# Second feed-forward: the down phase's second pass over 512 tokens becomes two passes over 256 tokens, and two more output tiles are finished under the last

## The chip, the cores and the metric

The kernel runs on one core of one Trainium2 chip. The metric is device time in microseconds (us): 3741.64 us median of 3 runs, 3740.01 to 3745.3. Engines are named as in the profile: PE (matrix multiplies), PEld (its weight loads), DVE (vector), ACT (scalar), POOL, and SP, the queue that issues the DMAs.

## The reference, cut to what matters

The program is a stack of two attention layers and a conditioned block of four stages. Only the last stage is touched: the second conv feed-forward, with its normalised, gated residual.

```python
D_MODEL, SEQ, D_FF = 1024, 1024, 2816
def conv_ffn(h, w_up, conv_w, conv_b, w_down):
    u = h @ w_up
    gate, val = u[..., :D_FF], u[..., D_FF:]
    gp = jnp.pad(gate, ((0, 0), (1, 1), (0, 0)))
    gate = gp[:, :-2] * conv_w[0] + gp[:, 1:-1] * conv_w[1] + gp[:, 2:] * conv_w[2] + conv_b
    return (jax.nn.silu(gate) * val) @ w_down
# end of the second block, per token:
x = x + gate_f * rmsnorm_2(conv_ffn(h, w_up[i], conv_w[i], conv_b[i], w_down[i]), g_post_ffn[i])
```

All of it is float32. The down product is hidden (1024 tokens by 2816) times w_down (2816 by 1024).

## The kernel before, in words

2816 is 22 chunks of 128 (`FT` = 22). The up phase computes each chunk of hidden, 128 channels by 1024 tokens, and stores it to memory outside the core (`hidden_dram`). The down phase reads it back and multiplies. A float32 operand is split into a high and a low part that the matrix unit takes, and a product is three matmuls: high by high, high by low, low by high.

**The down phase before** is two passes (h = 0, 1) over all 22 chunks. Pass h covers 512 tokens, that is 4 token tiles of 128, and both 512-column halves of the output; its 8 accumulators fill the 8 banks of `core.ps`. One step (h, f) is:
- SP loads chunk f of w_down (`down_raw`, 128 x 1024, 512 KB, L1793) and 512 tokens of hidden chunk f (`h_raw`, called hidden_columns in the trace, 256 KB, L1794). There are two slots for everything; s = f % 2.
- ACT copies both into high parts (`down_hi` L1888, `h_hi` L1889).
- DVE subtracts to get the low parts (`down_lo` L1972, `h_lo` L1974).
- PE runs 8 banks x 3 = 24 matmuls of 128x512 (L2070 to L2072).

**What sets the order.** The load for step n waits until DVE has finished the low parts of step n-2 (`down_lo` in `sync`), since these still read the raw slot. ACT's split of step n waits for both transfers of step n, and for PE to have finished step n-2 (`up_used`, or `acc` where n-2 ends a pass). PE's step n waits for DVE's low parts of step n. Every engine runs its instructions in program order. At a pass's end ACT evicts the even banks and DVE the odd ones into `y` (called x in the trace, L1941 and L2029); the next pass's first step waits for the eviction of each bank that it writes.

**The tail, class `Final`.** Each of 8 token tiles needs: ACT's sum of squares and mean (L2347, L2349), POOL's power -1/2 (L2363), DVE's scale (L2381) and addition of the old rows (L2383), and SP's store (L2331). Tiles 0 to 3 (`EARLY` = 4), complete after pass 0, are done in pass 1: ACT and POOL at steps 8 to 11, DVE at 10 to 13, the stores at 18 to 21. SP also loads the factor row at step 0 and one tile of old rows (512 KB each, L2324) at each of steps 0 to 7. Tiles 4 to 7 come after the last matmul.

Of the kernel before, what the change touches and what calls it, by code (L numbers as in the profile page):

```python
# [19 lines left out]
P = 128  # L20
# [1698 lines left out]
class FeedForward:  # L1719
# [12 lines left out]

    def __init__(self, core, combined, base, x_at, y, w_up, w_down, conv, hidden_dram, tail):
        self.core, self.combined, self.y, self.w_up, self.w_down = core, combined, y, w_up, w_down
# [43 lines left out]
    def sync(self, sp):  # L1778
        core, combined, cv, stored, final = self.core, self.combined, self.cv, self.stored, self.final

        def step(sp, f, s):
            if not final(f):
                sp.wait_ge(core.up_lo.sem, core.up_lo.at(3 * f + 3))
                combined.load(sp, self.w_up, f + 1)
            if not isinstance(f, int) or f > 0:
                sp.wait_ge(core.hidden.sem, core.hidden.at(f))
                sp.dma_start(self.hidden_dram[f - 1], cv[:, 1 - s]).then_inc(stored[1 - s].sem, 16)
        self.walk(sp, step)
        sp.wait_ge(core.up_lo.sem, core.up_lo.at(3 * FT))
# [12 lines left out]
        def down(h, f, s):  # L1802
            if h == 0 and isinstance(f, int) and f == FT - 2:
                sp.wait_ge(core.stored0.sem, core.stored0.at(8 * FT))
            if h == 0 and final(f):
                sp.wait_ge(core.stored1.sem, core.stored1.at(8 * FT))
            if h == 1 or not isinstance(f, int) or f > 1:
                sp.wait_ge(core.down_lo.sem, core.down_lo.at(2 * (h * FT + f) - 2))
                load(h, f, s)
        self.walk(sp, lambda sp, f, s: down(0, f, s))  # L1810
        for f in range(FT):
            down(1, f, f % 2)
            core.enter(self.tail.mark)
            self.tail.sync_early(sp, f)
            core.enter(self.mark)

# [25 lines left out]
    def gpsimd(self, pool):  # L1842
# [7 lines left out]
        self.walk(pool, step)  # L1850
        for f in range(FT):
            core.enter(self.tail.mark)
            self.tail.gpsimd_early(pool, f)
            core.enter(self.mark)
# [22 lines left out]
    def scalar(self, act):  # L1877
# [3 lines left out]
        def split(h, f, s):  # L1881
            n = h * FT + f
            act.wait_ge(downs[s].sem, downs[s].at(16 * (n - s) + 32))
            if h == 1 and isinstance(f, int) and f == 1:
                act.wait_ge(core.acc.sem, core.acc.at(8))
            else:
                need(act, core.up_used, FT - 1 if isinstance(f, int) and n == FT else n - 1 - h)
# [37 lines left out]
        def down(h, f, s):  # L1925
            if not final(f):
                split(h, f + 1, 1 - s)
            elif h == 0:
                split(1, 0, 0)
        for h in range(2):  # L1930
            if h == 0:
                self.walk(act, lambda act, f, s: down(0, f, s))
            else:
                for f in range(FT):
                    down(1, f, f % 2)
                    core.enter(self.tail.mark)
                    self.tail.scalar_early(act, f)
                    core.enter(self.mark)
            for b in range(0, 8, 2):
                act.wait_ge(core.acc.sem, core.acc.at(8 * h + b + 1))  # L1940
                act.activation(self.y[:, 4 * h + b // 2, 0:512], core.ps[:, b, :], ACT.Copy).then_inc(core.acc_used_act.sem, 1)  # L1941

# [21 lines left out]
    def vector(self, dve):  # L1964
# [4 lines left out]
        def split(h, f, s):  # L1969
# [3 lines left out]
            dve.wait_ge(core.down_hi.sem, core.down_hi.at(2 * n + 2))  # L1973
            dve.tensor_tensor(self.h_lo[:, s], self.h_raw[:, s], self.h_hi[:, s].bitcast(F32), ALU.subtract).then_inc(core.down_lo.sem, 1)  # L1974

# [37 lines left out]
        def down(h, f, s):  # L2013
            if not final(f):
                split(h, f + 1, 1 - s)
            elif h == 0:
                split(1, 0, 0)
        for h in range(2):
            if h == 0:
                self.walk(dve, lambda dve, f, s: down(0, f, s))  # L2020
            else:
                for f in range(FT):
                    down(1, f, f % 2)
                    core.enter(self.tail.mark)
                    self.tail.vector_early(dve, f)
                    core.enter(self.mark)
            for b in range(1, 8, 2):
                dve.wait_ge(core.acc.sem, core.acc.at(8 * h + b + 1))
                dve.tensor_copy(self.y[:, 4 * h + b // 2, 512:D], core.ps[:, b, :]).then_inc(core.acc_used_dve.sem, 1)  # L2029

    def tensor(self, pe):
# [25 lines left out]
        self.walk(pe, step)  # L2057
        for h in range(2):
            def down(pe, f, s):
                pe.wait_ge(core.down_lo.sem, core.down_lo.at(2 * (h * FT + f) + 2))  # L2060
                begin, end = isinstance(f, int) and f == 0, final(f)
                for b in range(8):
                    if begin and h == 0 and b % 4 == 0:
                        pe.wait_ge(core.parts_act.sem, core.parts_act.at(3 * (FT - 1 + b // 4)))
                        pe.wait_ge(core.parts_dve.sem, core.parts_dve.at(5 * (FT - 1 + b // 4)))
                    if begin and h == 1:
# [12 lines left out]
    def passed(self):  # L2079
        core = self.core  # L2080
        for c, n in ((core.raw0, 16 * FT), (core.up_hi, 3 * FT), (core.up_lo, 3 * FT), (core.weight_sums, 4 * FT), (core.products, 7 * FT),
                     (core.parts_act, 3 * FT), (core.parts_dve, 5 * FT), (core.gate_mid, FT), (core.gate_used, 2 * FT), (core.expo, FT),
                     (core.hidden, FT), (core.stored0, 8 * FT), (core.stored1, 8 * FT), (core.raw2, 32 * FT), (core.raw3, 32 * FT),
                     (core.down_hi, 4 * FT), (core.down_lo, 4 * FT), (core.up_used, 2 * (FT - 1)), (core.acc, 16),
                     (core.acc_used_act, 8), (core.acc_used_dve, 8)):
# [220 lines left out]
class Final:  # L2306

    def __init__(self, core, base, X, kept, factor_row, out):  # L2310
        self.core, self.X, self.kept, self.factor_row, self.out = core, X, kept, factor_row, out
# [6 lines left out]
    def sync_early(self, sp, f):  # L2318
# [14 lines left out]
    def sync(self, sp):  # L2333
        core = self.core
        for m in range(EARLY, TILES):
            self.store(sp, m)
# [14 lines left out]
    def scalar_early(self, act, f):  # L2351
        if 8 <= f < 8 + EARLY:
            self.scalar_tile(act, f - 8)

    def scalar(self, act):
        for m in range(EARLY, TILES):
            self.scalar_tile(act, m)
# [7 lines left out]
    def gpsimd_early(self, pool, f):  # L2365
        if 8 <= f < 8 + EARLY:
            self.gpsimd_tile(pool, f - 8)

    def gpsimd(self, pool):
        for m in range(EARLY, TILES):  # L2370
            self.gpsimd_tile(pool, m)
# [13 lines left out]
    def vector_early(self, dve, f):  # L2385
        if 10 <= f < 10 + EARLY:
            self.vector_tile(dve, f - 10)

    def vector(self, dve):
        for m in range(EARLY, TILES):  # L2390
            self.vector_tile(dve, m)
# [1004 lines left out]
def build(nc, I, out, stop=None):  # L3396

    with ExitStack() as ctx:
# [131 lines left out]

        def feed_forward(i, tail):
            conv = vec[:, VECTORS[f"conv{i}"]:VECTORS[f"conv{i}"] + 4 * FT].rearrange("p (a f) -> p a f", a=4)
            return FeedForward(core, combined[i], base, x_at, X, I["w_up"][i], I["w_down"][i], conv, hidden_dram, tail)
# [136 lines left out]
```

## Time and profile before

| | |
|---|---|
| median of 3 runs | 3741.64 us |
| profiled execution's own time | 3741.64 us |
| its span, first to last instruction | 3741.6 us |
| PE busy | 3430.4 us, 92% of the span |
| DVE, ACT, POOL busy | 2225.6, 1742.0, 1372.9 us |
| moved from and to memory | 269.76 MB read, 61.10 MB written |

The span and the profiled execution's own time agree, so a microsecond in the trace is one in the metric. Only the last 240 us are touched: the down phase of the second feed-forward runs from about 3484 to 3726 us, and the tail from there to the end. Matmuls are pipelined: one of 128x512 lasts 0.39 us in the trace, but the next starts 0.23 us after it, and that distance is what counts for a stream.

### The profile page before, as it was taken

Reading aid. Unit: us, or ns where it says so; the run is one execution under the profiler, and the core shown is the slowest. Engines: PE = TensorE matmul, PEld = TensorE weight load, DVE = VectorE, ACT = ScalarE, POOL = GpSimd, SP = SyncE. Lnnn points to the kernel's source line nnn. Section 1 sums busy time; section 2 is a strip of 40 time slices with the busy share of each in tenths; the row PEclk is TensorE's granted clock in tenths of the full one; section 3 lists DMA queues with packets and bytes.
Section 4 is the critical chain, followed back from the end, with each engine's and each line's share of the span. In section 5 each row is a group of like instructions: output and inputs, shape, how many; then the busy total and the mean of one; then the engine's idle time right before and its main releaser. Section 6 shows DMA issues by size and latency. Waiting matters only on the chain. (4 is left out here: it accounts for less than half of the span.)

```text
span 3741.6 us, 59020 instructions
## 1 busy us (share of the span) xinstructions
PE 3430.4 (92%) x18578; PEld 3015.6 (81%) x18578; DVE 2225.6 (59%) x4539; ACT 1742.0 (47%) x4132; POOL 1372.9 (37%) x1819
## 2 busy tenths in 40 slices
PE   5899989899999999797999939999998969999998
PEld 4799867899999997686998728888787758888786
DVE  5466777455677776435887186666435566666334
ACT  1277511767877772323665153333333463333333
POOL 2365433455566773313332224444001214444000
PEclk8999989999999998898999959999999779999999
DMA  3311255211212214300000022222364012222454
GB/s 137 140 39 41 97 230 225 88 43 42 60 60 64 64 61 169 131 1 29 1 0 0 34 107 85 84 80 83 126 205 140 34 57 80 80 82 84 138 194 146
DMA packets 97326, 332.99 MB, mean 89 GB/s; under 512 B 10705, under 2 KB 37633, under 8 KB 85122
## 3 DMA queue, kind: packets, MB, share of 16 engines
q1 hardware_dynamic: 97154, 330.90, 25.0%
q8 instruction: 83, 1.36, 0.2%
q14 instruction: 89, 0.73, 0.1%
HBM read 269.76 MB, written 61.10 MB: 88 GB/s over the span
## 5 line engine op out<-in xcount | busy, mean ns | idle before, releaser
L2070 PE MATMUL ps<-down_high,hidden_high 128*128 128x512 f32 x704 | 276.8, 393 | 15.0 <-DVE hidden_low L1974 14.6
L2071 PE MATMUL ps<-down_low,hidden_high 128*128 128x512 f32 x704 | 275.6, 391 | 0.0
L2072 PE MATMUL ps<-down_high,hidden_low 128*128 128x512 f32 x704 | 275.5, 391 | 0.0
L376 PE MATMUL ps<-w_hi,hT_hi 128*128 128x512 f32 x640 | 254.6, 398 | 22.0 <-DVE hT_lo L401 11.7
L1972 DVE TENSOR_TENSOR down_low<-down_raw,down_high 128x1024 fp32r<-128x1024 f32 x88 | 107.8, 1225 | 272.4 <-ACT down_high L1888 272.4
L2053 PE MATMUL ps<-columns_combined,up_high_even 128*128 128x512 f32 x616 | 242.6, 394 | 22.2 <-DVE columns_combined L2259 8.0
L377 PE MATMUL ps<-w_lo,hT_hi 128*128 128x512 f32 x640 | 253.4, 396 | 0.0
L378 PE MATMUL ps<-w_hi,hT_lo 128*128 128x512 f32 x640 | 253.0, 395 | 0.0
L2054 PE MATMUL ps<-columns_combined,up_high_even 128*128 128x512 f32 x616 | 241.8, 393 | 0.0
L2055 PE MATMUL ps<-columns_combined,up_low_even 128*128 128x512 f32 x616 | 241.6, 392 | 0.0
L2053 PE MATMUL ps<-columns_combined,up_high_odd 128*128 128x512 f32 x616 | 239.6, 389 | 0.0
L2054 PE MATMUL ps<-columns_combined,up_high_odd 128*128 128x512 f32 x616 | 239.6, 389 | 0.0
L2055 PE MATMUL ps<-columns_combined,up_low_odd 128*128 128x512 f32 x616 | 239.6, 389 | 0.0
L1092 ACT ACTIVATE masked_then_probs<-masked_then_probs,unit_rows 128x256 f32<-128x256 f32 (+1 forms) x512 | 229.1, 451 | 3.2 <-DVE sink_term L1179 1.8
L1888 ACT ACTIVATE down_high<-down_raw 128x1024 fp32r<-128x1024 f32 x88 | 93.1, 1058 | 269.3 <-PE ps L2072 256.4
L974 PE MATMUL ps<-w_units,hT_hi 128*128 128x384 f32 (+1 forms) x512 | 184.6, 361 | 22.3 <-DVE w_units L1138 16.6
L1029 PEld LDWEIGHTS ps<-v_tiles,probsT 128*128 128x128 f32 x1600 | 200.1, 195 | 1.4 <-issue 1.4
L976 PE MATMUL ps<-w_units,hT_lo 128*128 128x384 f32 (+1 forms) x576 | 198.9, 345 | 0.0
L1029 PE MATMUL ps<-v_tiles,probsT 128*128 128x64 f32 x1600 | 196.6, 274 | 0.8 <-DVE unit_rows L1252 0.8
L1170 DVE CUSTOM_DVE_ANT_0 masked_then_probs<-ps,mask 128x256 f32<-128x256 f32 (+1 forms) x512 | 156.1, 359 | 58.9 <-PE ps L991 58.6
L2491 DVE SCALAR_TENSOR_TENSOR mod_sums<-mod_weights,silu_c,mod_sums 128x512 f32 x196 | 182.4, 942 | 6.0
L974 PE MATMUL ps<-w_units,hT_hi_by_fours 128*128 128x384 f32 (+1 forms) x512 | 183.6, 359 | 0.0
(367 smaller groups left out, 9941.9 us busy)
## 6 DMA issues: line engine op xcount, KB each, us to landing
mod_weights<-in_w_mod SPq DMA_DIRECT2D x24, 2048.0 KB, 9.0
up_raw<-in_w_up SPq DMA_DIRECT2D x44, 1024.0 KB, 4.8
down_raw<-in_w_down SPq DMA_DIRECT2D x88, 512.0 KB, 3.6
hidden_columns<-hidden SPq DMA_DIRECT2D x44, 512.0 KB, 2.6
hidden_columns<-hidden_columns SPq DMA_DIRECT2D x88, 256.0 KB, 3.9
w_raw<-in_w_in_b SPq DMA_DIRECT2D x24, 768.0 KB, 4.5
group_rows<-unit_rows SPq DMA_DIRECT2D x64, 132.0 KB, 1.8
unit_rows<-group_rows SPq DMA_DIRECT2D x64, 132.0 KB, 2.1
```

Source lines behind the costliest of these rows:

```text
L376: nc.tensor.matmul(out, a, w_hi[:, s], start=(k == 0), stop=False)
L377: nc.tensor.matmul(out, a, w_lo[:, s], start=False, stop=False)
L378: last = nc.tensor.matmul(out, b, w_hi[:, s], start=False, stop=(k == KT - 1))
L974: nc.tensor.matmul(zbank, hi, weights(w_hi, a.unit, k), start=(k == 0), stop=False)
L1029: last = nc.tensor.matmul(o_bank[:, h * HD:(h + 1) * HD], pT[:, a.par, h, c], vs[:, tile], start=(c == a.slots[0]), stop=(c == a.slots[-1]))
L1092: act.activation(x, x, ACT.Exp, bias=own, scale=-1.0, accum_out=total).then_inc(core.probs.sem, 1)
L2053: nc.tensor.matmul(out, a_hi, combined.moving(0, z, k), start=(start and k == 0), stop=False, **again)
L2054: nc.tensor.matmul(out, a_hi, combined.moving(1, z, k), start=False, stop=False, **again)
L2055: last = nc.tensor.matmul(out, a_lo, combined.moving(0, z, k), start=False, stop=(k == 3), **again)
L2070: nc.tensor.matmul(out, h_hi[:, s, t], down_hi[:, s, cols], start=begin, stop=False)
L2071: nc.tensor.matmul(out, h_hi[:, s, t], down_lo[:, s, cols], start=False, stop=False)
L2072: last = nc.tensor.matmul(out, h_lo[:, s, t], down_hi[:, s, cols], start=False, stop=end)
```

## The change

The second feed-forward gets three passes instead of two. Pass 0 is as it was. Pass 1 covers tokens 512 to 767 in banks 0 to 3, pass 2 covers tokens 768 to 1023 in banks 4 to 7. Each of them walks all 22 chunks again: it loads the whole of chunk f of w_down and 256 tokens of hidden, splits them, and runs 12 matmuls a step. The steps of both are numbered through for the tail, 0 to 43. Tiles 4 and 5, complete after pass 1, are finished in pass 2: ACT and POOL at its steps 5 and 6, DVE at 7 and 8, the stores at 13 and 14. Tiles 6 and 7 remain for the end (`LATE` = 6). The first feed-forward keeps its two passes. Accumulators are counted so that pass 2 finds banks 4 to 7 evicted since pass 0.

```diff
+    HALVES = ((0, 512, 0, 8), (512, 512, 0, 8))
+    LAST_QUARTERS = ((0, 512, 0, 8), (512, 256, 0, 4), (768, 256, 4, 8))
...
             sp.dma_start(self.down_raw[:, s], self.w_down[f]).then_inc(self.downs[s].sem, 16)
-            sp.dma_start(self.h_raw[:, s], self.hidden_dram[f][:, 512 * h:512 * h + 512]).then_inc(self.downs[s].sem, 16)
+            first, n = self.passes[h][:2]
+            sp.dma_start(self.h_raw[:, s, 0:n], self.hidden_dram[f][:, first:first + n]).then_inc(self.downs[s].sem, 16)
...
-            if h == 1 or not isinstance(f, int) or f > 1:
+            if h >= 1 or not isinstance(f, int) or f > 1:
                 sp.wait_ge(core.down_lo.sem, core.down_lo.at(2 * (h * FT + f) - 2))
                 load(h, f, s)
         self.walk(sp, lambda sp, f, s: down(0, f, s))
-        for f in range(FT):
-            down(1, f, f % 2)
-            core.enter(self.tail.mark)
-            self.tail.sync_early(sp, f)
-            core.enter(self.mark)
+        for h in range(1, len(self.passes)):
+            for f in range(FT):
+                down(h, f, f % 2)
+                core.enter(self.tail.mark)
+                self.tail.sync_early(sp, (h - 1) * FT + f)
+                core.enter(self.mark)
...
-            if h == 1 and isinstance(f, int) and f == 1:
-                act.wait_ge(core.acc.sem, core.acc.at(8))
+            if h >= 1 and isinstance(f, int) and f == 1:
+                act.wait_ge(core.acc.sem, core.acc.at((8, 12)[h - 1]))
...
-            act.activation(self.h_hi[:, s], self.h_raw[:, s], ACT.Copy).then_inc(core.down_hi.sem, 1)
+            tokens = slice(0, self.passes[h][1])
+            act.activation(self.h_hi[:, s, tokens], self.h_raw[:, s, tokens], ACT.Copy).then_inc(core.down_hi.sem, 1)
...
-                for b in range(8):
+                for b in range(low, high):
...
-                    out, t, cols = core.ps[:, b, :], slice((b // 2) * P, (b // 2) * P + P), slice((b % 2) * 512, (b % 2) * 512 + 512)
+                    m = (b - low) // 2
+                    out, t, cols = core.ps[:, b, :], slice(m * P, m * P + P), slice((b % 2) * 512, (b % 2) * 512 + 512)
...
+    LATE = 6
...
-        if f >= FT - EARLY:
+        if FT - EARLY <= f < FT:
             self.store(sp, f - (FT - EARLY))
+        if f - FT in (13, 14):
+            self.store(sp, f - FT - 13 + EARLY)
...
+        if f - FT in (5, 6):
+            self.scalar_tile(act, f - FT - 5 + EARLY)
...
+        if f - FT in (7, 8):
+            self.vector_tile(dve, f - FT - 7 + EARLY)
...
-        second = feed_forward(1, final)
+        second = feed_forward(1, final, FeedForward.LAST_QUARTERS)
```

DVE's low parts and the evictions are cut to the pass's tokens and banks in the same way, and POOL's tiles 4 and 5 are placed as ACT's are.

**SP's queue** around the last steps of pass 1 (down_raw and hidden_columns are a step's two loads, out_x is the store of a finished tile). Before:

```order
L2331 DMA out_x<-x 128x1024 [waits x_new]
L1793 DMA down_raw_21217<-in_w_down 128x1024 [waits down_lo]
L1794 DMA hidden_columns_21220<-hidden_columns 128x512
L2331 DMA out_x<-x 128x1024 [waits x_new] x5
L3352 UNCONDITIONAL_BRANCH [waits loads]
```

The same place now, and the first steps of pass 2 behind it:

```order
L2345 DMA out_x<-x 128x1024 [waits x_new]
L1797 DMA down_raw_21217<-in_w_down 128x1024 [waits down_lo]
L1799 DMA hidden_columns_21220<-hidden_columns 128x256
L1797 DMA down_raw_21217<-in_w_down 128x1024 [waits down_lo]
L1799 DMA hidden_columns_21220<-hidden_columns 128x256
```

Before, five stores and the end followed the last load; now 22 more pairs of loads follow the fourth store, and each pair waits for DVE's low parts of two steps earlier. The weight load kept its width, the token load has half.

**DVE's queue** at the end of the program (COPY is an eviction, the two rows behind it are the scale and the addition of one tile). Before:

```order
L1972 TENSOR_TENSOR down_low_21219<-down_raw_21217,down_high_21218 128x1024 [waits down_hi]
L1974 TENSOR_TENSOR hidden_low_21222<-hidden_columns_21220,hidden_high_21221 128x512 [waits down_hi]
L2029 COPY x<-ps 128x512 [waits acc] x4
L2381 SCALAR_TENSOR_TENSOR x<-x,statistics,final_factor 128x1024 [waits y_rstd,ready1]
L2383 TENSOR_TENSOR x<-x,final_old_rows 128x1024 [waits y_scaled]
```

And the end of the first of the two short passes, where DVE has two evictions, with the next pass behind it:

```order
L1979 TENSOR_TENSOR down_low_21219<-down_raw_21217,down_high_21218 128x1024 [waits down_hi]
L1982 TENSOR_TENSOR hidden_low_21222<-hidden_columns_21220,hidden_high_21221 128x256 [waits down_hi]
L2037 COPY x<-ps 128x512 [waits acc] x2
L1979 TENSOR_TENSOR down_low_21219<-down_raw_21217,down_high_21218 128x1024 [waits down_hi]
L1982 TENSOR_TENSOR hidden_low_21222<-hidden_columns_21220,hidden_high_21221 128x256 [waits down_hi]
```

Before, the four evictions were followed by four tiles of two instructions each (the fence shows the first); now two evictions stand in the middle and two at the end, two tiles have moved up into pass 2, and two are left behind the last eviction.

## Rows read from the trace of the kernel before

**Rows 1.** Table by stretches: PE busy (instructions), granted clock, DMA share, GB/s
```profile
core 0: us, PE busy (x), PEclk, DMA share, GB/s
3500.00:3594.00 94.00, 94.00 (x416) 1.00 0.44 148
3600.00:3632.00 32.00, 32.00 (x143) 1.00 0.73 250
...
3607.00:3726.00 119.00, 119.00 (x527) 1.00 0.52 174
```

**Rows 2.** The chain that ended last: start, length, what
```profile
3725.94 0.04 ACT x L1941
3725.99 0.45 issue
3726.44 1.15 ACT final_squares L2347 x2
...
3728.70 1.29 DVE x L2381
...
3737.38 1.22 DVE x L2383
```

**Rows 3.** Timeline of SP, two issues of the loads
```profile
3642.59 0.33 SPq L1793 DMA_DIRECT2D down_raw<-in_w_down  x1
3642.96 0.43 SPq L1794 DMA_DIRECT2D hidden_columns<-hidden_columns  x1
```

**Rows 4.** Timeline of ACT, same step
```profile
3639.64 1.06 ACT L1888 ACTIVATE down_high<-down_raw 128x1024 fp32r<-128x1024 f32 x1 [3.86 <-PE ps L2072]
3640.61 0.61 ACT L1889 ACTIVATE hidden_high<-hidden_columns 128x512 fp32r<-128x512 f32 x1
3645.08 1.06 ACT L1888 ACTIVATE down_high<-down_raw 128x1024 fp32r<-128x1024 f32 x1 [3.86 <-PE ps L2072]
```

**Rows 5.** Timeline of DVE, the same step, and one with a tile
```profile
3640.73 1.23 DVE L1972 TENSOR_TENSOR down_low<-down_raw,down_high 128x1024 fp32r<-128x1024 f32 x1 [3.61 <-ACT down_high L1888]
3641.88 0.68 DVE L1974 TENSOR_TENSOR hidden_low<-hidden_columns,hidden_high 128x512 fp32r<-128x512 f32 x1
...
3664.24 1.28 DVE L2381 SCALAR_TENSOR_TENSOR x<-x,statistics,final_factor 128x1024 f32<-128x1024 f32 x1
3665.55 1.22 DVE L2383 TENSOR_TENSOR x<-x,final_old_rows 128x1024 f32<-128x1024 f32 x1
```

**Rows 6.** Landing of the 39 weight loads L1793, from 3500 us on
```profile
L1793 SPq DMA_DIRECT2D down_raw<-in_w_down x39: 327/328/339, 3500.1 to 3707.9; - x39
...
DMA to landing us min/median/max: 3.2/3.6/4.1
```

**Rows 7.** Landing of the 39 token loads L1794, from 3500 us on
```profile
L1794 SPq DMA_DIRECT2D hidden_columns<-hidden_columns x39: 332/433/598, 3500.6 to 3708.2; - x39
...
DMA to landing us min/median/max: 3.5/3.9/4.9
```

**Rows 8.** The chain of waits where pass 0 starts
```profile
3490.34 4.43 DMA hidden_columns<-hidden_columns
3494.77 0.02 issue
3494.79 1.07 ACT down_high L1888
3495.86 0.02 issue
3495.89 0.57 DVE down_low L1972
...
3497.03 0.69 DVE hidden_low L1974
3497.72 0.04 issue
3497.77 0.50 PE ps L2070
```

**Rows 9.** Table by stretches, a crowded queue, and PE with gaps at either clock
```profile
412.00:429.00 17.00, 13.60 (x113) 1.00 0.08 25
1842.00:1853.00 11.00, 9.47 (x68) 1.00 0.00 0
3059.40:3064.30 4.90, 4.90 (x12) 0.50 0.00 0
3489.80:3496.40 6.60, 6.12 (x27) 1.00 0.92 318
```

More of the change, by code:

```diff
@@ L1731, with __init__ @@
              (6, 2, 2, False, 2), (3, 4, 3, True, 3))
-    def __init__(self, core, combined, base, x_at, y, w_up, w_down, conv, hidden_dram, tail):
+    HALVES = ((0, 512, 0, 8), (512, 512, 0, 8))
+    LAST_QUARTERS = ((0, 512, 0, 8), (512, 256, 0, 4), (768, 256, 4, 8))
+    def __init__(self, core, combined, base, x_at, y, w_up, w_down, conv, hidden_dram, tail, passes=HALVES):
+        self.passes = passes
         self.core, self.combined, self.y, self.w_up, self.w_down = core, combined, y, w_up, w_down
@@ L1850, in gpsimd @@
         self.walk(pool, step)
-        for f in range(FT):
+        for f in range((len(self.passes) - 1) * FT):
             core.enter(self.tail.mark)
@@ L1927, in down @@
                 split(h, f + 1, 1 - s)
-            elif h == 0:
-                split(1, 0, 0)
-        for h in range(2):
+            elif h < len(self.passes) - 1:
+                split(h + 1, 0, 0)
+        for h, (first, n, low, high) in enumerate(self.passes):
             if h == 0:
@@ L1934, in scalar @@
                 for f in range(FT):
-                    down(1, f, f % 2)
+                    down(h, f, f % 2)
                     core.enter(self.tail.mark)
-                    self.tail.scalar_early(act, f)
+                    self.tail.scalar_early(act, (h - 1) * FT + f)
                     core.enter(self.mark)
-            for b in range(0, 8, 2):
-                act.wait_ge(core.acc.sem, core.acc.at(8 * h + b + 1))
-                act.activation(self.y[:, 4 * h + b // 2, 0:512], core.ps[:, b, :], ACT.Copy).then_inc(core.acc_used_act.sem, 1)
+            for b in range(low, high, 2):
+                act.wait_ge(core.acc.sem, core.acc.at((8 if h else 0) + b + 1))
+                act.activation(self.y[:, first // P + (b - low) // 2, 0:512], core.ps[:, b, :], ACT.Copy).then_inc(core.acc_used_act.sem, 1)
     def first_sums(self, dve, early=False):
@@ L1973, in split @@
             dve.wait_ge(core.down_hi.sem, core.down_hi.at(2 * n + 2))
-            dve.tensor_tensor(self.h_lo[:, s], self.h_raw[:, s], self.h_hi[:, s].bitcast(F32), ALU.subtract).then_inc(core.down_lo.sem, 1)
+            tokens = slice(0, self.passes[h][1])
+            dve.tensor_tensor(self.h_lo[:, s, tokens], self.h_raw[:, s, tokens], self.h_hi[:, s, tokens].bitcast(F32), ALU.subtract).then_inc(core.down_lo.sem, 1)
         def step(dve, f, s):
@@ L2015, in down @@
                 split(h, f + 1, 1 - s)
-            elif h == 0:
-                split(1, 0, 0)
-        for h in range(2):
+            elif h < len(self.passes) - 1:
+                split(h + 1, 0, 0)
+        for h, (first, n, low, high) in enumerate(self.passes):
             if h == 0:
@@ L2022, in vector @@
                 for f in range(FT):
-                    down(1, f, f % 2)
+                    down(h, f, f % 2)
                     core.enter(self.tail.mark)
-                    self.tail.vector_early(dve, f)
+                    self.tail.vector_early(dve, (h - 1) * FT + f)
                     core.enter(self.mark)
-            for b in range(1, 8, 2):
-                dve.wait_ge(core.acc.sem, core.acc.at(8 * h + b + 1))
-                dve.tensor_copy(self.y[:, 4 * h + b // 2, 512:D], core.ps[:, b, :]).then_inc(core.acc_used_dve.sem, 1)
+            for b in range(low + 1, high, 2):
+                dve.wait_ge(core.acc.sem, core.acc.at((8 if h else 0) + b + 1))
+                dve.tensor_copy(self.y[:, first // P + (b - low) // 2, 512:D], core.ps[:, b, :]).then_inc(core.acc_used_dve.sem, 1)
     def tensor(self, pe):
@@ L2057, in tensor @@
         self.walk(pe, step)
-        for h in range(2):
+        for h, (first, n, low, high) in enumerate(self.passes):
             def down(pe, f, s):
@@ L2334, in sync @@
         core = self.core
-        for m in range(EARLY, TILES):
+        for m in range(self.LATE, TILES):
             self.store(sp, m)
@@ L2353, in scalar_early @@
             self.scalar_tile(act, f - 8)
+        if f - FT in (5, 6):
+            self.scalar_tile(act, f - FT - 5 + EARLY)
     def scalar(self, act):
-        for m in range(EARLY, TILES):
+        for m in range(self.LATE, TILES):
             self.scalar_tile(act, m)
@@ L2367, in gpsimd_early @@
             self.gpsimd_tile(pool, f - 8)
+        if f - FT in (5, 6):
+            self.gpsimd_tile(pool, f - FT - 5 + EARLY)
     def gpsimd(self, pool):
-        for m in range(EARLY, TILES):
+        for m in range(self.LATE, TILES):
             self.gpsimd_tile(pool, m)
@@ L2387, in vector_early @@
             self.vector_tile(dve, f - 10)
+        if f - FT in (7, 8):
+            self.vector_tile(dve, f - FT - 7 + EARLY)
     def vector(self, dve):
-        for m in range(EARLY, TILES):
+        for m in range(self.LATE, TILES):
             self.vector_tile(dve, m)
@@ L3529, in build, with feed_forward @@
         combined = [Combined(core, base) for _ in range(2)]
-        def feed_forward(i, tail):
+        def feed_forward(i, tail, passes=FeedForward.HALVES):
             conv = vec[:, VECTORS[f"conv{i}"]:VECTORS[f"conv{i}"] + 4 * FT].rearrange("p (a f) -> p a f", a=4)
-            return FeedForward(core, combined[i], base, x_at, X, I["w_up"][i], I["w_down"][i], conv, hidden_dram, tail)
+            return FeedForward(core, combined[i], base, x_at, X, I["w_up"][i], I["w_down"][i], conv, hidden_dram, tail, passes)
         final = Final(core, base, X, x_dram, rows_dram[4], out)
-        second = feed_forward(1, final)
+        second = feed_forward(1, final, FeedForward.LAST_QUARTERS)
         pool = PoolMix(core, base, x_at, X, x_dram, rows_dram, I, pre_ffn[1][:], mod[1][:, 24:32], second)
```

9 lines of the change are left out of this document (5 added, 4 removed).

## Prediction

> **What bounds the kernel now.** I read first the table by stretches, since the change touches only the last 240 us. In it the reader is to see that PE is busy for the whole of each stretch, 94.00 of 94.00 and 119.00 of 119.00 us, at clock 1.00 [rows 1]. So the down phase is bound by PE alone: 527 matmuls in 119 us are 0.226 us each, a step of 24 is 5.44 us, and pass 1 is 22 x 5.44 = 119.7 us. Then the chain that ended last: after the last evictions it holds only the tail, ACT's squares from 3726.44, DVE's first scale at 3728.70, then eight DVE instructions back to back until 3738.6 [rows 2], and the last store, with the span's end at 3741.6. One tile costs DVE 3664.24 to 3665.55 and some 1.15 more, 2.45 us [rows 5]; in the tail the last addition starts at 3737.38 and the first scale at 3728.70, which gives (3737.38 + 1.22 - 3728.70)/4 = 2.475 a tile [rows 2]. Last, what feeds PE: the timelines of SP, ACT and DVE for one step and the landings of its two transfers [rows 3 to 7]. There ACT and DVE wait 3.86 and 3.61 us per step, ACT for PE: everything that prepares a step has slack today, because PE takes 5.44 us for it. That slack is what the change spends.
>
> **The tail: a gain of 4.9 us.** Four tiles behind the last eviction become two. ACT's last eviction, its squares, POOL and DVE's first scale follow each other as now, so the start of DVE's run keeps its distance from the last matmul, and its run is two tiles shorter: 2 x 2.475 = 4.9 us. The last store lands 3.0 us after DVE as now (3741.6 - 3738.6).
>
> **PE's own work: zero.** 44 steps of 12 matmuls are the 528 of 22 steps of 24. Pass 2 writes banks 4 to 7, evicted since pass 0, so it waits for no eviction. If PE were still the bound, these passes would again take 119.7 us.
>
> **Feeding PE: the large term.** A step now lasts PE 12 x 0.227 = 2.72 us, but it still needs the whole 512 KB of w_down, ACT's 128x1024 copy and DVE's 128x1024 subtraction. Only the token part is halved. With two slots the load of step n+2 is issued when DVE has finished the low parts of step n, so one turn of a slot is a closed loop in which PE has no part:
> - DVE's end to SP's issue: 3641.88 + 0.68 = 3642.56 to 3642.59, 0.03 us [rows 5, 3].
> - Issue to both landed: the weights land 3.6 us after their issue [rows 6]. The tokens are issued 0.37 later [rows 3] and land 3.9 after that [rows 7], at 4.27. So the 256 KB add 0.67, and I take half of it for 128 KB: 3.6 + 0.33 = 3.93.
> - Landing to ACT's copy 0.02 [rows 8]; ACT's start to DVE's start 3640.73 - 3639.64 = 1.09 [rows 4, 5]; DVE's first subtraction to its second 1.15 [rows 5].
> - The second subtraction has 256 columns. From 1.23 us for 1024 columns and 0.68 for 512 [rows 5] the slope is 0.55 per 512, so 0.68 - 0.27 = 0.41.
>
> The turn is 0.03 + 3.93 + 0.02 + 1.09 + 1.15 + 0.41 = 6.63 us for two steps, 3.3 a step where PE needs 2.72. The loop was there before, with 6.63 + 0.34 + 0.27 = 7.24 us for two steps, under PE's 10.88. That it can be last is seen where pass 0 starts: the chain runs through the transfer (4.43 us), ACT, DVE, PE [rows 8].
>
> Bounds of the landing: the least token landing is 3.5 and the greatest 4.9 [rows 7], so both have landed after 3.5 + 0.37 - 0.33 = 3.54 or 4.94, which is 6.24 or 7.64 a turn, 3.12 or 3.82 a step. If halving the tokens saves nothing, 4.27 gives 3.5. I take the median, 3.3.
>
> **The sum of the two passes.** Steps 0 to 2 were fed during pass 0 and run at PE's pace, 8.2 us; the load of step 3 needs the low parts of step 1, which need the last matmul of pass 0: 2.7 (ACT and DVE) + 3.95 (landing) + 2.7 = 9.4 us until PE starts step 3. The 40 intervals to the start of step 43 at 3.31 are 132.6, the last step 2.7: together 144.7. On top:
> - DVE in the six steps with a tile: 1.15 + 0.33 (0.41 less the 0.08 by which DVE's instructions overlap, 1.23 against 1.15) + 2.45 = 3.93, longer than 3.31, with the next subtraction queued behind the tile and SP's next load waiting for it: 6 x 0.62 = 3.7 us.
> - The transfers of old rows at pass 1's steps 0 to 7: a step moves 512 + 128 + 512 KB, 1.18 MB. In the crowded stretch the queue moved 318 GB/s [rows 9], so 3.7 us a step, 0.4 above 3.31. Before, the same extras were hidden: PE 32.00 of 32.00 us at 250 GB/s [rows 1]. Six intervals lie behind step 3: 2.4 us. The six stores are as large; I take half of their 2.4, since a transfer to memory delays only the weights behind it: 1.2.
>
> That is 144.7 + 3.7 + 2.4 + 1.2 = 152.0 us against 119.7: a loss of 32.3. With the tail: 32.3 - 4.9 = +27.4. The profiled execution took 3741.6 us, the same as the median, so 3741.6 + 27.4 = 3769; the queue's extras may partly coincide with DVE's, so I forecast 3768 us.
>
> A page bears on the landing. "DMA: Bandwidth & Descriptors", section "Anatomy of one DMA", of the Trainium skill gives some 2.0 us fixed plus bytes over 436 GB/s; for this pair of 655,360 bytes an estimate by it is 3.5 us in place of 3.93, 6.2 us a turn, and about 3760 us. It was fitted on another engine's path, and by it the pair of today, 786,432 bytes, would land after 3.8 where the rows show 4.27; the rows decide.
>
> **Rivals.**
> 1. **The loads stay hidden, PE stays the bound.** The two passes take 119.7 us and the tail's 4.9 come off whole: 3736.7, and with one start-up gap of 1.2 (9.4 - 8.2) about 3738, faster. For it: PE never waits in either pass today [rows 1], and the queue's share is 0.44 to 0.52. It needs a turn below 5.44 us. Against it: without any transfer the turn is 2.7 us, so the pair would have to land within 2.74 us of its issue, and the fastest of 39 weight loads alone took 3.2 [rows 6]. Chance 4%.
> 2. **Crowded queue.** If every transfer lands as late as the latest today, 3.82 a step: 9.4 + 152.8 + 2.7 + 3 = 167.9, that is +43.3, 3785. For it: twice the weight bytes per us, some 640 KB in 3.3 us, 200 GB/s against 148 in quiet steps [rows 1]. Against it: at 250 GB/s PE did not wait at all, and 318 were reached. Chance 12%.
> 3. **PE's clock falls.** With gaps of 0.6 us in every 3.3, PE is busy for 82%. At the lower level 12 matmuls filled 4.9 us at a granted 0.50 [rows 9], so the half level of 1.2 GHz makes PE the bound again: 44 x 4.9 = 216, and 3741.6 + 216 - 119.7 - 4.9 = 3833. Against it: with 13.60 of 17.00 us busy, 80%, and 9.47 of 11.00, the clock stayed at 1.00 [rows 9]. Chance 4%. "TensorE: Matmul & The Clock Gate", section "HAM oscillation", of the Trainium skill speaks for this rival: matmul bursts with waits for transfers between them can each start at the half clock. The waits here are shorter than in its example, and the rows above show none of it.
> 4. **The loop at its best.** 3.12 a step and no extra but DVE's: 9.4 + 124.8 + 2.7 + 3.7 = 140.6, +16, 3757.6. Chance 15%.
>
> **How the numbers follow.** The forecast, the loop of load, ACT, DVE and load at about 3.3 us a step, has 65%, with 3761 to 3776 as its own range; the rivals above have 35%. The range is 3755 to 3782: it takes in the best loop and most of the way to the crowded queue, and leaves out rival 1, rival 3 and the worst of rival 2. A measurement of this kernel tells about 0.2%, 7.5 us. Only rival 1 ends below or near the old time: 2% for faster by more than that, 2% for within it (rival 1's 3738 lies inside 0.2%, but without the start-up gap and with a little more from the tail it may reach beyond), 96% for slower.
>
> **What would show it.** In the changed profile: PE waits at the first matmul of nearly every step of passes 1 and 2 for DVE's hidden_low; ACT's down_high waits for the transfer and no longer for PE; steps are 3.1 to 3.5 us apart, 3.7 to 3.9 where a tile or old rows are; PE's clock stays at 1.00; first DVE scale of the last tiles some 2.3 us behind the last matmul as now, and two tiles, not four, behind it. I am wrong if ACT still waits for PE in these passes, if the weights land under 2.7 us, or if the granted clock falls.

## The result and the profile after

| | before | changed |
|---|---|---|
| median | 3741.34 us (4 runs, 3740.01 to 3745.3) | 3771.23 us (4 runs, 3767.9 to 3773.41) |
| profiled span | 3741.6 us | 3766.1 us |
| PE busy | 3430.4 us | 3436.6 us |
| read from memory | 269.76 MB | 281.29 MB |

The ratio is 1.0078, 95% interval 1.0064 to 1.0093: 30 us slower, where the forecast was 3768 us in 3755 to 3782. A second set of five runs beside other runs of the kernel before gave 3771.36 us and 1.0081 (1.0068 to 1.0095). One of the ten executions of a variant below (e6) took 12320.87 us at a mean granted clock of 0.267; it is left out, and e6's median is that of the other nine.

One correction to the table before: in every later profiled execution the time is about 1.8 us above the span (3767.9 and 3766.1), so equal numbers for the kernel before are doubtful by as much. Stretches of the trace are safer than spans here. Nothing ahead of pass 1 was changed, yet in the profiles below that leave pass 0 alone its last eviction starts anywhere between 3598.9 and 3609.2 us. I therefore measure passes 1 and 2 from the start of DVE's last eviction of pass 0 to the start of its last of all. In the timeline of DVE (start, length, what, and in brackets the wait before it and what ended it) the kernel before has

```profile
3606.94 0.69 DVE L2029 COPY x<-ps 128x512 f32<-128x512 f32 x1 [0.38 <-PE ps L2072]
...
3726.62 0.69 DVE L2029 COPY x<-ps 128x512 f32<-128x512 f32 x1 [0.67 <-PE ps L2072]
```

and the changed kernel

```profile
3604.40 0.69 DVE L2037 COPY x<-ps 128x512 f32<-128x512 f32 x1 [0.65 <-PE ps L2081]
...
3756.06 0.69 DVE L2037 COPY x<-ps 128x512 f32<-128x512 f32 x1 [0.69 <-PE ps L2081]
```

That is 119.68 us against 151.66, a loss of 31.98. Below, "the passes" is always this stretch. The tail from there, in the chain that ended last:

```profile
3755.87 1.15 ACT final_squares L2361 x2
...
3758.06 1.29 DVE x L2399
3759.38 1.23 DVE x L2401
3760.61 1.21 DVE x L2399
3761.84 1.23 DVE x L2401
```

Four DVE instructions in the chain where there were eight [rows 2]. From that last eviction to the span's end it is 3766.1 - 3756.06 = 10.0 us, before it was 3741.6 - 3726.62 = 15.0. Read to the end of DVE's last addition, in hundredths, it is 7.01 us against 11.98 [rows 2], which is 4.97 less. The two stretches together give 31.98 - 4.97 = +27.0 us.

Where the 32 us went is shown by the table of waits inside the passes (who waited for whom: total us, times, longest):

```profile
ACT down_high L1894 <- DMA hidden_columns<-hidden_columns: 78.0, 40, 3.0
PE ps L2079 <- DVE hidden_low L1982: 20.5, 29, 1.3
ACT down_high L1894 <- PE ps L2081: 1.4, 1, 1.4
```

ACT waits 40 times for the transfer and once for PE; before it waited for PE, 3.86 us a step [rows 4]. And the chain that ended last, which held only PE in this stretch before, is now the slot's loop (start, length, what):

```profile
3733.35 0.33 SPq L1797
...
3733.72 3.40 DMA hidden_columns<-hidden_columns
...
3737.14 1.07 ACT down_high L1894
...
3738.23 1.23 DVE down_low L1979
3739.46 0.35 DVE hidden_low L1982
3739.82 0.33 SPq L1797
...
3746.45 0.33 SPq L1797
```

The same slot's load is issued at 3733.35, 3739.82 and 3746.45: 6.47 and 6.63 us for two steps, with PE nowhere in them. I call this distance, from the issue of the weights of step n to that of step n+2, the turn of step n (steps 0 to 43 of passes 1 and 2). Some turns hold extra work, and I group them by it: 3 to 9 lie beside the loads of old rows, 12 to 15 and 31, 32 behind a tile on DVE, 19 to 23 and 36 to 38 beside a store. The 18 others from 3 to 41 I call plain. The two slots turn independently, so the steps are not evenly spaced: behind step 3 the issues follow each other after 2.4 to 4.4 us. The table by stretches answers to [rows 1]:

```profile
core 0: us, PE busy (x) PEld busy (x) DVE busy (x) ACT busy (x) POOL busy (x), PEclk, DMA share, GB/s
3606.00:3757.00 151.00, 129.30 (x521) 94.36 (x519) 83.23 (x102) 68.44 (x108) 4.15 (x6) 1.00 0.68 218
```

PE is busy 129.30 of 151 us, at the full clock of 2.4 GHz (granted 1.00) throughout.

### The profile page after: what moved, and what is told of

Same layout as the page of the kernel before. It is cut to its first block and busy times, and to the rows that moved or that the text cites. A ratio compares the mean times of both kernels' runs of the same rounds, so it can differ in the third digit from the quotient of the medians.

```text
span 3766.1 us, 59212 instructions
## 1 busy us (share of the span) xinstructions
PE 3436.6 (91%) x18578; PEld 3009.3 (80%) x18578; DVE 2255.8 (60%) x4583; ACT 1766.6 (47%) x4176; POOL 1368.9 (36%) x1819
## 3 DMA queue, kind: packets, MB, share of 16 engines
HBM read 281.29 MB, written 61.10 MB: 91 GB/s over the span
## 5 line engine op out<-in xcount | busy, mean ns | idle before, releaser
L1979 DVE TENSOR_TENSOR down_low<-down_raw,down_high 128x1024 fp32r<-128x1024 f32 x110 | 134.7, 1225 | 274.9 <-ACT down_high L1894 274.9
L1894 ACT ACTIVATE down_high<-down_raw 128x1024 fp32r<-128x1024 f32 x110 | 116.4, 1059 | 277.0 <-PE ps L2081 184.6
L2079 PEld LDWEIGHTS ps<-down_high,hidden_high 128*128 128x128 f32 x704 | 133.2, 189 | 83.0 <-DVE hidden_low L1982 55.4
```

## The experiments

All start from the changed kernel. Passes are in us from one profile each. Two variants do not compute the product any more: e2 multiplies whatever weights the slots still hold, and e9 multiplies tokens 512 to 767 again in pass 2.

| run | edit | passes | median, ratio to before (interval) |
|---|---|---|---|
| changed, a2 | none | 151.66 and 152.80 | 3771.23, 1.0078 (1.0064 to 1.0093); 3771.36, 1.0081 (1.0068 to 1.0095) |
| e1 | tiles 4, 5 at the end | 151.57 | 3772.31, 1.0079 (1.0064 to 1.0094) |
| e2 | no weights loaded | 134.04 | 3751.12, 1.0022 (1.0012 to 1.0032) |
| e3 | three raw slots | 134.13 | 3752.12, 1.0027 (1.0017 to 1.0038) |
| e4 | old rows in pass 0 | 151.87 | 3770.69, 1.0075 (1.0059 to 1.009) |
| e5 | half tiles | 152.97 | 3771.21, 1.0076 (1.0061 to 1.0091) |
| e8 | e4 and e5 | 146.77 | 3765.18, 1.0061 (1.0046 to 1.0077) |
| e9 | 512 tokens loaded | 161.20 | 3780.65, 1.0101 (1.0086 to 1.0117) |
| e10 | tokens counted apart | 147.72 | 3764.55, 1.006 (1.0044 to 1.0075) |
| e6 | three slots for loads and parts | 122.80 | 3740.42, 0.9996 (0.9986 to 1.0006) |
| e7 | e6, e4, e5 | 120.12 and 121.70 | 3738.47, 0.9989 (0.998 to 0.9998); 3737.75, 0.9984 (0.9975 to 0.9993) |

### a2: the changed kernel again

No edit; it gives the spread of one profile.

> The changed kernel once more, on the same chip as the next three, to have its passes and its time beside theirs. Passes 1 and 2, from the last eviction of pass 0 to the last eviction of the end, took 151.7 us in its first profile: between 150 and 153 again, tail 10.5 us, about 27 us slower than the kernel before.

The passes took 3756.18 - 3603.38 = 152.80 us, 1.1 more than in the first profile, and 3766.2 - 3756.18 = 10.0 us lie behind them. Below, differences under 2 us between single profiles say nothing.

### e1: the tail alone

```diff
-    LATE = 6
+    LATE = 4
...
-        if f - FT in (7, 8):
-            self.vector_tile(dve, f - FT - 7 + EARLY)
```

with the tiles' ACT, POOL and store calls taken out in the same way.

> The changed kernel with tiles 4 and 5 finished at the end again, behind the last matmul. Theory (slot loop plus a shorter tail): the tail is 4.9 us longer, two of the six steps that DVE stretches to 3.93 us are back at 3.3 (-1.2), so 3.7 us slower than the changed kernel, about 3775 us; between DVE's first scale of the end and its last addition 9.8 us instead of 4.9. Rival (the work moved under the pass costs there as much as it saves at the end): no difference, 3771.

In the chain of waits of this run the tail is

```profile
3757.88 1.29 DVE x L2393
...
3766.55 1.22 DVE x L2395
```

eight instructions, 3766.55 + 1.22 - 3757.88 = 9.89 us against 5.01 in the changed kernel (3758.06 to 3763.07). So the move is worth 4.9 us at the end. The rival was that the two tiles cost as much under pass 2. Then e1's passes would be 4.9 us shorter than the changed kernel's; they took 151.57 us against 151.66 and, in a2, 152.80. The 1.2 us that they were to lose did not show in the sum either. It shows in the turns: those of steps 31 and 32, behind the two tiles, took 7.59 and 7.85 us and now 6.59 and 6.60, which is 1.1 us over both, since a turn covers two steps. In this one profile the turns beside old rows and stores were slower by more than that (7.37 and 7.23 us on the mean against 7.06 and 7.05 in the first profile). The time was expected at 3775 us; the medians (3772.3 and 3771.2, from different chips) do not resolve 5 us between them, and the trace does.

### e2: without the weights' transfer

```diff
-            sp.dma_start(self.down_raw[:, s], self.w_down[f]).then_inc(self.downs[s].sem, 16)
+            if not short:
+                sp.dma_start(self.down_raw[:, s], self.w_down[f]).then_inc(self.downs[s].sem, 16)
```

> The changed kernel, but passes 1 and 2 load only the 256 tokens of a step (128 KB) and no weights: the 512 KB of w_down are left out, everything else runs on what the slots hold. Theory (the weights' transfer is the long part of the slot's turn): a landing of about 2.2 us instead of 3.93 makes the turn 4.9 us, under PE's 5.44, so steps of 2.8 us, 3.9 where DVE has a tile: the two passes take about 128 us instead of 149, time about 3750. Rival A (ACT's and DVE's preparation of a step is the bound, whatever the transfer): no change, 3771. Rival B (PE itself is slowed by waiting and restarting at each step): no change either, steps stay at 3.3.

The 40 token loads landed in

```profile
DMA to landing us min/median/max: 2.2/2.3/2.5
```

and the passes fell from 152 to 134.04 us. The median fell to 3751, as expected, but the passes were expected at 128; the plain turns are 5.83 us here as in e3, where the reason shows. In the waits ACT waited for PE again, 36 times between 3608 and 3726 us. So ACT's and DVE's preparation is not the bound at 3.3 us a step, and PE's restarts are not either: the transfer is the long part of the loop.

### e3: the same bytes, a third raw slot

```diff
+            self.down_raw_third = place("down_raw_third", [P, D], F32, base + 11 * RKB)
+            self.h_raw_third = place("hidden_columns_third", [P, 512], F32, base + 12 * RKB)
...
-                sp.wait_ge(core.down_lo.sem, core.down_lo.at(2 * (h * FT + f) - 2))
+                sp.wait_ge(core.down_lo.sem, core.down_lo.at(2 * (h * FT + f) - (4 if h and len(self.passes) == 3 else 2)))
```

> The changed kernel with a third slot for the loaded data of passes 1 and 2 (weights and tokens); high and low parts keep two slots. The same bytes are moved. Theory (a closed loop of load, ACT, DVE with two slots, bound by latency): the turn of 6.6 us now covers three steps, 2.2 a step, so the next bound shows: ACT may write the high parts of step n+2 only when PE is done with step n, 2.85 + 2.72 us for two steps, 2.8 a step; with 3.7 where old rows are loaded (8 steps) and 3.9 at DVE's tiles (6 steps) the passes take about 137 us instead of 149: time about 3759. Rival (the queue is bound by bytes, 640 KB in 3.3 us): the same bytes in the same time, no change, 3771.

The passes took 134.13 us, the same as without the weights. Over the passes the queue moved 240 GB/s where it had 221, so bytes did not bind in the changed kernel. What bound was the length of the loop, divided by only two slots. In the timeline of ACT the next bound shows:

```profile
3607.50 1.06 ACT L1913 ACTIVATE down_high<-down_raw 128x1024 fp32r<-128x1024 f32 x1 [1.35 <-PE ps L2101]
...
3610.61 1.06 ACT L1913 ACTIVATE down_high<-down_raw 128x1024 fp32r<-128x1024 f32 x1 [1.74 <-PE ps L2101]
...
3613.33 1.06 ACT L1913 ACTIVATE down_high<-down_raw_third 128x1024 fp32r<-128x1024 f32 x1 [1.35 <-PE ps L2101]
```

Steps are 3.11 and 2.72 us apart in turn, and ACT waits for PE each time: 5.83 us for two steps, where I had reckoned 5.57. This next loop is ACT, DVE, then PE's step, then ACT again. The chain that ended last shows which part I had too short:

```profile
3712.80 1.07 ACT down_high L1913
...
3715.51 0.50 PE ps L2099
...
3718.67 1.07 ACT down_high L1913
```

From ACT's start to PE's first matmul it is 2.71 us (reckoned 2.85), but from there to ACT's next start 3.16, where I had put PE's 2.72. In PE's timeline the first two matmuls after the wait are 0.34 us apart and the twelfth starts 2.67 us after the first, in place of 11 x 0.227 = 2.50; it then lasts its full 0.40 us before ACT may start. The steps with old rows, which I had put at 3.7 us, run at this same pace, so that the passes came out at 134 us and not at the 137 expected.

### e4, e5 and e8: the two extras

e4 calls `old_rows(sp, f - 4)` after each step of pass 0 instead of in pass 1. e5 splits a tile:

```diff
-        if 10 <= f < 10 + EARLY:
-            self.vector_tile(dve, f - 10)
...
+        if 10 <= f < 10 + 2 * EARLY:
+            self.vector_tile(dve, (f - 10) // 2, f % 2)
...
```

The last argument chooses the half: the scale in one step, the addition in the next. Tiles 4 and 5 are split in the same way over steps 7 to 10 of pass 2. e8 makes both edits.

> The changed kernel with the factor and the eight tiles of old rows loaded in pass 0 (steps 4 to 11) instead of pass 1 (steps 0 to 7). Theory (the prediction's term for the crowded queue): passes 1 and 2 lose 2.4 us, 149.3 instead of 151.7; pass 0 stays at PE's pace, since the same load beside 5.44 us steps cost nothing in the kernel before. Rival (the steps with old rows were 3.45 us on average in the changed kernel's profile, little over the others, so the term was too large): passes about 150.5 to 151.5. Rival B (pass 0 begins to wait): PE's gaps in pass 0 grow.

> The changed kernel with DVE's two instructions of each early tile in two successive steps (tiles 0 to 3 over steps 10 to 17 of pass 1, tiles 4 and 5 over steps 7 to 10 of pass 2). Theory (the prediction's term of 3.7 us: six steps at 3.93 instead of 3.31): 1.15 + 0.33 + 1.31 = 2.8 us of DVE a step is under the loop's 3.3, no step is set by DVE's total any more, though each half tile may push the split behind it by up to 1.3 us: passes 148.0 instead of 151.7. Rival (a half tile before the split of every second slot delays the closed loop by its own length, in twelve steps instead of six): no gain, 151 to 154. What speaks for the rival: with two tiles fewer in the passes, the run with four tiles at the end took 151.6, no less.

> The changed kernel with both edits of the two runs before: old rows loaded in pass 0, and DVE's tiles in halves. Either edit alone left the passes at 151.9 and 153.0 us, though the turns of the steps concerned fell (7.1 to 7.7 us down to 6.6). Theory (the two extras are real and each was covered by slower landings at the stores in those two executions): passes 152 - 1.6 to 3.8 - 2 = about 147 us, all turns but those at stores at 6.6. Rival (what one step loses to a tile or a crowded queue is made up or lost elsewhere in the closed loop, so that the sum stays): 151 or more.

Alone, neither moved the passes (151.87 and 152.97 us), so both expectations (149.3 and 148.0) missed, and e5 came out where its rival put it. Together they took 4.9 to 6.0 us off (146.77), as expected. In each alone the turns concerned did fall. Beside the old rows the mean turn is 7.06 and 7.69 us in the two profiles of the changed kernel and 6.61 in e4. Behind the tiles it is 7.72 and 7.56, and 6.50 in e5. Nor did the halves cost there what the rival said: the turns behind them (steps 12 to 18 and 31 to 34) are 6.60 us on the mean. But the turns at the stores were slower in these two executions, 7.40 and 7.88 against 7.05 and 6.96. Pass 0 did not pay for the old rows in e4: between 3500 and 3594 us PE was busy for 94.00 us. Without an edit the tile steps look like this in SP's timeline, every issue waiting for DVE's split behind a tile, 3.92 us apart:

```profile
3645.46 0.33 SPq L1797 DMA_DIRECT2D down_raw<-in_w_down  x1
...
3649.38 0.33 SPq L1797 DMA_DIRECT2D down_raw<-in_w_down  x1
...
3653.31 0.33 SPq L1797 DMA_DIRECT2D down_raw<-in_w_down  x1
```

So both terms exist and their sum is about right, 5.5 measured (152.2 - 146.8, the mean of the two profiles less e8's) against 6.1 predicted. Why a single edit's gain went to the stores is open; one profile each does not tell chance from cause.

### e9: 128 KB more in the loop

```diff
+            if n < 512:
+                first, n = 512, 512
```

> The changed kernel, but every step of passes 1 and 2 loads 512 tokens of hidden (256 KB, tokens 512 to 1023) instead of its 256, and uses the first 256; pass 2 therefore multiplies the tokens of pass 1 again. Nothing else differs: a dose of 128 KB more in the loop. Theory (slot loop): the landing is 4.27 us instead of 3.93, as in the kernel before, the turn 6.97 instead of 6.63: 0.17 us a step, the passes 6 to 8 us longer, 158 to 160 us. Rival A (the loop is bound by latency alone, and bytes behind the weights cost nothing): 152. Rival B (bytes bind: 20% more of them): 152 x 1.2 = 180.

The passes took 161.20 us, 9 more, against 6 to 8 expected and 0 or 28 by the rivals. The median plain turn is 6.87 us instead of 6.62, which is 0.25 more where 0.34 was expected. At the stores and old rows it is more (8.1 and 7.7 on the mean, against 7.05 and 7.06). In this run the longer load cost most where the queue was already crowded. A token load took up to

```profile
DMA to landing us min/median/max: 3.6/3.9/6.6
```

### e10: ACT starts when the weights have landed

```diff
+            if self.short(h):
+                act.wait_ge(core.tokens[s].sem, core.tokens[s].at(8 * (n - FT - s) + 16))
             act.activation(self.h_hi[:, s, tokens], self.h_raw[:, s, tokens], ACT.Copy)
```

and the weights' wait counts them alone.

> The changed kernel with a counter of their own for the tokens of passes 1 and 2, so that ACT copies the weights as soon as they have landed, and waits for the tokens only before it copies these. Theory (slot loop, of which the wait for the later of the two transfers is a part): the weights land 3.5 us after their issue where both have landed after 3.95, so the turn is 0.4 us shorter, 6.2, the steps 3.1 us, the passes 152 - 7 = about 145 us, the time about 3764. Rival (the weights' data, not the tokens, are what ACT waited for, as they land last or the tokens land with them): 152, no change.

In the waits inside the passes ACT's releaser is now the weights' transfer:

```profile
ACT down_high L1901 <- DMA down_raw<-in_w_down: 73.6, 40, 3.7
```

The passes took 147.72 us, 4.5 less where 7 less was expected; the median is 3764.55, as expected. The median plain turn is 6.28 us against 6.62, most of the 0.4 expected. The rival, no change, is out: the wait for the later transfer was part of the loop.

### e6 and e7: three slots for the parts too

e6 adds to e3 a third `down_high`, `down_low`, `hidden_high` and `hidden_low`, and issues ACT's and DVE's splits two steps ahead; e7 adds the edits of e4 and e5.

```diff
+            self.thirds = [place("down_high_third", [P, D], F32R, base + 13 * RKB), place("down_low_third", [P, D], F32R, base + 14 * RKB),
+                           place("hidden_high_third", [P, 512], F32R, base + 15 * RKB), place("hidden_low_third", [P, 512], F32R, base + 16 * RKB)]
...
+            done = n - 3
...
```

> The third slot for loaded data and also for the high and low parts, splits two steps ahead, but the old rows stay in pass 1 and DVE's tiles stay whole: the kernel with everything less the last two edits. Theory: with a third slot for the parts the alternation 2.72 / 3.11 us of the version with three raw slots goes (ACT no longer waits for PE to finish the step before last), so plain steps are 2.72; the eight steps with old rows are bound by 1.18 MB at 318 GB/s, 3.7 us, less what the slots hold in stock; the six tile steps by DVE, 3.93, less the stock: 119.7 + 5 + 5 = about 130 us, against 134.1 with three raw slots and 120.1 with everything. Rival (the third slot for the parts is worth nothing and the whole gain from 134.1 to 120.1 is the other two edits): 134.

> Three slots for the loaded data and for the high and low parts in passes 1 and 2, splits issued two steps ahead, the old rows and the factor loaded in pass 0 (steps 4 to 11), and DVE's two instructions of a tile put into two successive steps. Theory: every loop is then under PE's 2.72 us a step, DVE needs 1.15 + 0.33 + 1.31 = 2.8 in the tile steps, the queue 640 KB in 2.7 us, 240 GB/s, where 318 were seen: the passes take about 121 us, and with the short tail the time is 3741.3 + 1.3 - 4.9 = 3738 us, about 0.1% faster than the kernel before and 33 us faster than the changed one. Rival (the queue cannot deliver 640 KB every 2.72 us beside its latency, or the clock or PE's restarts cost): steps of 3.0 us or more, 3750 or more.

> The version with three slots everywhere, old rows in pass 0 and half tiles, once more for its verdict: passes 120 us, 3 to 6 us under the kernel before (ratio 0.9985).

e6: 122.80 us. The third slot for the parts, with the splits two steps ahead, takes 134.1 to 122.8, better than the 130 expected. The price I had put on tiles and old rows, 5 us each, was too high: most of their delay is covered by what three slots hold ready. The table by stretches shows where the rest is, the first stretch being old rows and tiles:

```profile
3612.00:3660.00 48.00, 46.17 (x203) 37.46 (x202) 34.09 (x41) 27.12 (x45) 3.53 (x4) 1.00 0.83 279
3660.00:3727.00 67.00, 66.77 (x295) 54.78 (x294) 43.43 (x55) 35.73 (x56) 1.10 (x2) 1.00 0.76 244
```

e7 closes the gap in that first stretch: PE is busy for 48.00 of 48.00 us there in both its profiles. In the first, PE is busy all the time again:

```profile
3612.00:3729.00 117.00, 116.86 (x516) 96.42 (x515) 79.97 (x98) 65.00 (x104) 4.90 (x6) 1.00 0.77 246
```

The passes took 120.12 us in this profile and 121.70 in the next against 119.68 before, with a tail 5 us shorter. In the second, PE waited once, for 1.7 us, at the first step of pass 2. In the first it waited once for as long between 3500 and 3520 us, in pass 0, where the old rows are now loaded. What the last two edits add to e6 (1.1 and 2.7 us of passes) is hardly more than single profiles differ. Its medians, 3738.47 and 3737.75 us, are 5.5 and 4.4 us under those of the kernel before beside them (3743.98 and 3742.18), both intervals below 1: faster than the kernel before by 0.11 and 0.16%. That is what the change could be worth with one more slot throughout.

## Why the prediction was right

- **Tail, -4.9.** Measured -4.97 (11.98 to 7.01 us to DVE's last end), and e1 shows it alone: 9.89 against 5.01 us of DVE.
- **PE's own work, zero.** Right: the clock was 1.00 throughout, and in e7 the 44 steps take 120.12 and 121.70 us where the 22 took 119.68.
- **The slot's turn, 6.63 us.** The term that carries the forecast. From the timelines of SP, ACT and DVE of the changed kernel, the median of the 18 plain turns is 6.62 (mean 6.67), of which issue to ACT's start 3.94 (forecast 3.95). The weights landed 3.5 us after their issue (forecast 3.6), the tokens 3.6 after their own (3.57), both medians of the first profile:

```profile
L1799 SPq DMA_DIRECT2D hidden_columns<-hidden_columns x40: 333/433/548, 3610.2 to 3746.8; - x40
...
DMA to landing us min/median/max: 3.2/3.6/5.1
```

  The half-size subtraction took 0.42 (0.41). e2, e3, e9 and e10 changed one part of the loop each, and each moved the passes the way the loop says, by -18, -18, +9 and -4.5 us. One sign that I had named was too strong: PE waits 29 times, not at nearly every one of the 44 steps; successive loads are issued 2.4 to 4.4 us apart, and a step that follows closely is ready when PE is.
- **The extras.** By the turns (half of what a turn has above the plain mean, for each turn of its group), in the changed kernel's two profiles: DVE's tiles 3.2 and 2.6 us (forecast 3.7), old rows 1.4 and 3.5 (2.4), stores 1.5 and 1.1 (1.2). Tiles and old rows together are 5.5 by e8 against 6.1. The reason I gave for halving the stores' term, that a transfer to memory delays only the weights behind it, no run tests; in e4, e5, e8 and e9 the turns at the stores were 7.3 to 8.1 us on the mean, so that term is the least certain.
- **The sum** was 152.0 us for the passes; measured 151.66 and 152.80. That it is so close owes something to luck: single extras were off by up to 1.1 us in either direction and partly cancelled, and my 40 intervals used the median turn where the mean was 0.05 higher, 1 us in all.
- **The time.** 3768 against 3771.2. The trace's two stretches give +27.0, forecast +27.4; the medians differ by 30, with an interval of 24 to 35. The remaining 3 us are not resolved: the profiled time of the kernel before is doubtful by 1.8 us, and what lies ahead of pass 1 moves by more.
- **The rivals.** Loads stay hidden: excluded by the waits, 40 of 41 for the transfer. Crowded queue: a token load took up to 5.1 us to land, but from issue to ACT's start it was 4.1 us on the mean and 4.2 in a2, not 4.94. The clock: granted 1.00 with PE busy 86% of the time; the longest of PE's 29 waits was 1.3 us (2.4 in a2), and none lowered it. The loop at its best: it needs a turn of 6.24 us with both transfers landed after 3.54, and in the first profile the earliest start of ACT was 3.60 after the issue.
- **The Trainium skill.** Its fit ("DMA: Bandwidth & Descriptors", "Anatomy of one DMA") gave an estimate of 3.5 us for the pair. The rows gave 3.94 to ACT's start, so the measurement decides; the estimate's 3760 us is 11 short of the 3771 measured. Its account of bursts that each start at the half clock ("TensorE: Matmul & The Clock Gate", "HAM oscillation") speaks of longer waits than these, and this trace shows none of it: the granted clock stayed at 1.00 through all 29 waits.

The weakest step was the next bound in e2 and e3: 2.8 us a step expected, 2.92 found. I had put PE's step at its streaming time of 2.72 us in a loop where 3.16 us lie between its first matmul and what waits for its last.

## What to carry to other kernels

Halving the work per load does not halve the load: before cutting a pass, walk one buffer slot round its loop (free, issue, landing, every engine that reads it, free) and divide by the number of slots; if that exceeds the consumer's new step, the loop is the time, however idle each engine and the queue look. The cure here was a slot more at every stage of the loop, since a third slot for the loads alone only handed the bound to the next pair of buffers. When a loop includes the matrix unit, count its step from the first matmul to the end of the last, not at the streaming distance. When effects are a few us in 3700, measure a stretch between two events in the trace, not the span.

## What the runs showed of the hardware

- With no weight load in the queue, a 128 KB load landed 2.3 us after its issue (e2, median of 40). In the changed kernel a 512 KB load landed after 3.5 and the 128 KB behind it after 3.6 of its own. Where 512 KB of old rows was queued as well (steps 4 to 7), ACT started 4.4 to 5.1 us after the issue of the weights, and in a2 up to 6.45.
- One core's queue of SP carried 246 GB/s for 117 us with PE busy throughout (e7), against 218 over 151 us when two slots limited the requests.
- After a wait the first two matmuls are 0.33 to 0.34 us apart instead of 0.23. In the changed kernel PE was not the bound and this cost nothing visible; in e3 PE's step is part of the loop, and its twelve starts took 2.67 us instead of 2.50, of 5.83 for two steps.
- Waits of up to 1.3 us, 29 of them in 151 us with PE busy 86% of the time, left the granted clock at 1.00, the level of 2.4 GHz.
